# First expert's rows by one-hot products, router on un-normalised rows, bias split and table steps moved

## The reference, cut to what matters

```
h = h + mixed @ w_out
hn = rms_norm(h, norm_ffn_g)                       # h * rstd * g
logits = hn @ router_w + router_b
top_vals, top_idx = top_k(logits, 4); gates = softmax(top_vals)
# tokens sorted by expert, in blocks of 128
gu = x @ w_gate_up[e] + b_gate_up[e]
gate, lin = min(gu[:, 0::2], 7), clip(gu[:, 1::2], -7, 7)
act = gate * sigmoid(1.702 * gate) * (lin + 1)
y = act @ w_down[e] + b_down[e]                    # times the gate, added to h
```

## Time and profile before

| what | value |
|---|---|
| time, median of 3 runs | 1485.84 us (1485.42 to 1486.91) |
| profiled execution, its own time | 1486.37 us |
| its span | 1484.7 us |
| PE busy | 1418.3 us (96%) |
| DVE busy | 1235.6 us (83%) |
| ACT busy | 1006.7 us (68%) |
| POOL busy | 264.8 us (18%) |
| granted TensorE clock, mean | 0.966 |

### The profile page before, as it was taken

One profiled execution on the slowest core, in us unless ns is written; L12 is line 12 of the kernel. 1 busy time (PEld: TensorE's weight loads), 2 busy tenths in 40 slices (PEclk: granted clock), 3 DMA queues, 4 the chain that ended last, 5 costly groups with the idle time before them and its releaser, 6 DMA issues.

```text
span 1484.7 us, 20096 instructions
## 1 busy us (share of the span) xinstructions
PE 1418.3 (96%) x6498; PEld 1143.8 (77%) x6498; DVE 1235.6 (83%) x1074; ACT 1006.7 (68%) x1014; POOL 264.8 (18%) x280
## 2 busy tenths in 40 slices
PE   6998969879999999999999999999999999999995
PEld 4887447766888888888888888888888888888884
DVE  4688665566999999999989999999999999989994
ACT  5248265443777777777777777777777777777773
POOL 3000000054011112211211111122221122221111
PEclk9999979867999999999999999999999999999998
DMA  7412003658999999999999999999999999999971
GB/s 242 151 55 85 1 1 126 240 132 284 353 380 364 380 381 368 369 377 372 373 364 373 371 364 371 384 358 369 386 358 382 370 357 369 377 374 369 367 292 21
DMA packets 96842, 445.74 MB, mean 300 GB/s; under 512 B 14895, under 2 KB 19007, under 8 KB 63920
## 3 DMA queue, kind: packets, MB, share of 16 engines
q1 hardware_dynamic: 82752, 421.82, 75.2%
q0 software_dynamic: 11392, 17.61, 5.0%
q10 hardware_dynamic: 2672, 5.99, 1.3%
HBM read 439.96 MB, written 22.43 MB: 311 GB/s over the span
## 4 chain that ended last, share of the span: by engine, by line
PE 93%; DVE 3%; ACT 1%; DMA 1%; issue 1%; SPq 0%; POOL 0%; ACTq 0%; POOLq 0%; DVEq 0%
PE psum L1318 27%; PE psum L1319 27%; PE psum L1320 27%; PE psum L1609 2%; PE psum L1403 2%; PE psum L1618 2%; PE psum L1635 1%; DMA ring<-in_w_in 1%; PE psum L1644 1%; PE psum L1538 1%; PE psum L1476 1%; PE psum L1417 0%; DVE wlo L1215 0%; PE psum L1436 0%; PE psum L1556 0%
## 5 line engine op out<-in xcount | busy, mean ns | idle before, releaser
L1215 DVE TENSOR_TENSOR wlo<-ring,whi 128x2048 fp32r<-128x2048 f32 x384 | 871.6, 2290 | 109.7 <-ACT whi L783 105.9
L783 ACT ACTIVATE whi<-ring 128x2048 fp32r<-128x2048 f32 x384 | 737.2, 1920 | 195.0 <-PE psum L1320 195.0
L1318 PE MATMUL psum<-whi,xT_hi 128*128 128x512 f32 x1024 | 403.6, 394 | 6.2 <-DVE wlo L1215 3.4
L1319 PE MATMUL psum<-whi,xT_lo 128*128 128x512 f32 x1024 | 400.5, 391 | 0.0
L1320 PE MATMUL psum<-wlo,xT_hi 128*128 128x512 f32 x1024 | 400.3, 391 | 0.0
L1318 PEld LDWEIGHTS psum<-whi,xT_hi 128*128 128x128 f32 x1024 | 193.6, 189 | 46.7 <-DVE wlo L1215 3.8
L1320 PEld LDWEIGHTS psum<-wlo,xT_hi 128*128 128x128 f32 x1024 | 193.5, 189 | 40.5
L1319 PEld LDWEIGHTS psum<-whi,xT_lo 128*128 128x128 f32 x1024 | 193.6, 189 | 39.1
L1318 PE MATMUL psum<-whi,aT_hi 128*128 128x512 f32 x512 | 202.0, 395 | 1.9 <-ACT y_sb L809 1.9
L1320 PE MATMUL psum<-wlo,aT_hi 128*128 128x512 f32 x512 | 199.6, 390 | 0.0
L1319 PE MATMUL psum<-whi,aT_lo 128*128 128x512 f32 x512 | 199.5, 390 | 0.0
(11 more groups left out here) (241 smaller groups left out, 1356.4 us busy)
## 6 DMA issues: line engine op xcount, KB each, us to landing
ring<-in_w_gate_up SPq DMA_DIRECT2D x256, 1024.0 KB, 7.6
ring<-in_w_down SPq DMA_DIRECT2D x128, 1024.0 KB, 7.0
ring<-in_w_in SPq DMA_DIRECT2D x10, 1024.0 KB, 11.3
ring<-in_w_out SPq DMA_DIRECT2D x4, 1024.0 KB, 4.9
h<-in_x SPq DMA_DIRECT2D x4, 512.0 KB, 5.7
hn_rows<-hn ACTq DMA_DIRECT2D x4, 512.0 KB, 3.2
out<-h ACTq DMA_DIRECT2D x4, 512.0 KB, 8.2
bias_rows<-rows_st SPq DMA_DIRECT2D x1, 1280.0 KB, 4.8
```

Source lines behind the costliest of these rows:

```text
L783: nc.scalar.activation(whi[:, hi_of(number), :], ring[:, slot(number), :], ACT.Copy).then_inc(hi_ready, 1)
L1215: TT(wlo[:, slot(number), :], ring[:, slot(number), :], whi[:, hi_of(number), :].bitcast(F32), ALU.subtract).then_inc(lo_ready, 1)
L1318: MM(o, s_hi, m_hi, start=first, stop=False)
L1319: MM(o, s_lo, m_hi, start=False, stop=False)
```

## The change

- **Rows of item 0.** They are no longer gathered from HBM and transposed. DVE writes `sel_rows[:, t, :]` (128 x 128: token p of tile t is at place c of expert 0) and PE forms the transposed rows as `hn[:, t, d].T @ sel_rows[:, t]`, 8 float32 products of 128 columns for each tile. The gathers on POOL begin with item 1.
- **Router.** PE transposes `h1` instead of `hn`; `router_w` is multiplied by the norm's gain once (an extra small load, `gffn_k`), and `choose` multiplies the logits by `rstd2` while it adds the router's bias.
- **Ranks** are fp32r products of `mask_r`, `tri_r`, `ones_r`.
- **Up bias.** Loaded early on ACT's queue into ring slot 4, split (ACT line "b_split", DVE `bias_low` twice) into ring slot 5 between `add_rest(0)`, `(1)` and `(2)`, then moved by a POOL DMA to `b_hl`. Loads 10 and 11 of the ring wait for it.
- **Table steps, places, dense gates** come after `lo_item(0, 2)` and later, with the PE steps of them between the `use_up`; the transposes of the gates come after `bias_up(0)`, and ACT's evacuation of them after its last up chunk.

```diff
@@ ScalarE
             act.dma_start(g_ffn[:, :], norm_ffn_g.partition_broadcast(P)).then_inc(g_ffn_loaded, 16)
+            for part in range(4):
+                act.dma_start(b_raw[part * E:(part + 1) * E, :], b_gate_up).then_inc(braw_loaded, 16)
...
+            act.wait_ge(bhl_one, 1)
+            nc.scalar.activation(b_split[:, :], b_raw[:, :], ACT.Copy).then_inc(bhl_hi, 1)
             root(0)
             root(1)
...
             act.wait_ge(chunk_used, N_FRONT)
+            act.dma_start(b_dn[:, :], b_down).then_inc(b_dn_loaded, 16)
             gates_exp(1)
+            hi_item(0, 0)
+            hi_item(0, 1)
             gates_exp(2)
+            hi_item(0, 2)
             gates_exp(3)
...
-            for k in range(FIRST_HI):
+            xgT_out(0)
+            hi_item(0, FIRST_HI)
+            hi_item(0, FIRST_HI + 1)
+            for k in range(FIRST_HI + 2, UP):
                 hi_item(0, k)
             act.wait_ge(gdT_done, 1)
+            act.wait_ge(hn_stored, 16 * T)
-            nc.scalar.activation(gateT[:, :, :], bank(7)[0:E, :].rearrange("p (t c) -> p t c", t=T),
+            nc.scalar.activation(gateT[:, :, :], bank(4)[0:E, :].rearrange("p (t c) -> p t c", t=T),
                                  ACT.Copy).then_inc(gdT_evac, 1)
-            xgT_out(0)
-            act.wait_ge(braw_loaded, 80)
-            act.wait_ge(bhl_one, 1)
-            act.wait_ge(hn_stored, 16 * T)
-            nc.scalar.activation(b_hl[:, :], b_raw[:, :], ACT.Copy).then_inc(bhl_hi, 1)
-            for k in range(FIRST_HI, UP):
-                hi_item(0, k)
             hi_item(0, UP + 0)
             hi_item(0, UP + 1)
             sigmoid(0)
@@ VectorE
+            TT(rw[:, :, :], rw[:, :, :], gffn_k.unsqueeze(2).to_broadcast([P, KT, E]), ALU.mult).then_inc(rw_scaled, 1)
...
+            def position(t):
...
+                link(TT(pos[:, t, :], bank(RANKS[t])[:, 0:E], row_e[:, :], ALU.add))
+                TS(sel_rows[:, t, :], place_no[:, 0, :], pos[:, t, 0:1], mask[:, t, 0, 0:1], ALU.is_equal,
+                   ALU.mult).then_inc(rows_chosen, 1)
+            def next_lists():
+                for t in range(T):
+                    for e in range(1, AHEAD):
+                        TS(sel0[:, t, e - 1, :], place_no[:, e, :], pos[:, t, e:e + 1], mask[:, t, 0, e:e + 1], ALU.is_equal,
+                           ALU.mult).then_inc(sel0_ready, 1)
+            def one_more():
+                dve.wait_ge(braw_loaded, 64)
+                linear = b_raw[:, :].rearrange("p (f two) -> p two f", two=2)[:, 1, :]
+                TS(linear, linear, 1.0, None, ALU.add).then_inc(bhl_one, 1)
+            def bias_low(low):
+                dve.wait_ge(bhl_hi, 1)
+                TT(b_split[low, :], b_raw[low, :], b_split[low, :].bitcast(F32), ALU.subtract).then_inc(bhl_ready, 1)
+            one_more()
+            add_rest(0)
+            normalise(0)
+            bias_low(slice(E, 2 * E))
+            add_rest(1)
+            normalise(1)
+            bias_low(slice(3 * E, P))
+            add_rest(2)
+            normalise(2)
+            choose(0)
+            add_rest(3)
+            normalise(3)
+            position(0)
+            choose(1)
+            choose(2)
+            position(1)
+            choose(3)
+            position(2)
+            position(3)
+            lo_item(0, 0)
+            split_xgT(0)
+            lo_item(0, 1)
+            next_lists()
+            lo_item(0, 2)
+            dve.wait_ge(slot0_done, 1)
+            TS(slot0_i[:, 1:AHEAD], bank(4)[:, 497:496 + AHEAD], float(NOWHERE), None, ALU.add).then_inc(slot0_ready, 1)
...
+            lo_item(0, 3)
+            flags()
+            lo_item(0, 4)
+            place(0)
             places()
+            lo_item(0, 5)
+            place(1)
             items()
+            lo_item(0, 6)
+            place(2)
+            place(3)
+            dense_gates(0)
+            dense_gates(1)
+            pick(0, sel_up, sel_up_ready, None)
+            lo_item(0, 7)
+            dense_gates(2)
+            dense_gates(3)
             lo_item(0, UP + 0)
             clip(0)
@@ TensorE
+            def first_rows(t):
+                pe.wait_ge(rows_chosen, t + 1)
+                pe.wait_ge(hn_ready, t + 1)
...
+                for half in range(2):
+                    for k in range(4):
+                        d = (half * 4 + k) * P
+                        ins = MM(bank(6 + half)[:, k * P:(k + 1) * P], hn[:, t, d:d + P], sel_rows[:, t, :],
+                                 start=(t == 0 and k == 0), stop=(t == T - 1 and k == 3))
...
+            turn_h1(1)
             out_rows(3)
             ranks(0)
+            turn_h1(2)
             logits(1)
+            turn_h1(3)
+            logits(2)
             ranks(1)
             logits(3)
+            first_rows(0)
             ranks(2)
+            first_rows(1)
             ranks(3)
+            first_rows(2)
+            first_rows(3)
...
             pe.wait_ge(xgT_ready, 2)
             for k in range(UP):
                 use_up(0, k, k)
+                if k == 1:
+                    for t in range(T):
+                        first_slots_of(t)
+                if k == 2:
+                    counts()
+                if k == 3:
+                    prefix()
+                if k == 4:
+                    item_table()
+            pe.wait_ge(bhl_moved, 16)
             bias_up(0)
+            turn_gates()
+            pe.wait_ge(items_ready, 1)
+            pe.wait_ge(gdT_evac, 1)
+            pe.wait_ge(b_dn_loaded, 16)
             for t in range(T):
                 bias_down(t)
@@ GpSimd and SyncE
+            pool.wait_ge(logits_done, T)
+            pool.wait_ge(bhl_ready, 2)
+            pool.dma_start(b_hl[:, :], b_split[:, :]).then_inc(bhl_moved, 16)
+            pool.wait_ge(sel0_ready, T * (AHEAD - 1))
             nc.gpsimd.memset(xg[:, :], 0.0).then_inc(xg_cleared, 1)
             pool.wait_ge(slot0_ready, 1)
-            gather(0, slot0_i[:, 0:1])
-            scatter_rows(0)
-            scatter_rows(1)
             gather(1, slot0_i[:, 1:2])
-            scatter_rows(2)
-            scatter_rows(3)
+            for t in range(T):
+                scatter_rows(t)
             gather(2, slot0_i[:, 2:3])
...
                 if m == PER_ITEM - 3:
                     sp.wait_ge(hn_stored, 16 * T)
+                if m == PER_ITEM - 2:
+                    sp.wait_ge(bhl_ready, 2)
                 if m == PER_ITEM - 1:
-                    sp.wait_ge(xg_loaded, 16)
+                    sp.wait_ge(bhl_moved, 16)
```

More of the change, by code:

```diff
@@ L115, in build @@
         eps, spare = vecs[:, 23:24], vecs[:, 29:30]
+        gffn_k = vecs[:, 30:38]
         lam2, rlam = vecs[:, 24:26], vecs[:, 26:28]
@@ L450, in _ @@
                 small(sg, subln_g.rearrange("(p a) -> p a", a=1))
+                small(gffn_k, norm_ffn_g.rearrange("(k p) -> p k", p=P))
             small(rw[:, :, :], router_w.rearrange("(k p) e -> p k e", p=P))
@@ L754, in gates_exp, with hi_item @@
                                      accum_out=gates[:, t, 5:6]).then_inc(gate_exp, 1)
+            def hi_item(body, number):
+                act.wait_ge(slot_loaded[slot(number)], loads(body, number))
+                act.wait_ge(chunk_used, chunk(body, number) - HI + 1)
+                nc.scalar.activation(whi[:, hi_of(number), :], ring[:, slot(number), :], ACT.Copy).then_inc(hi_ready, 1)
             root(0)
@@ L1208, in _ @@
-            flags()
-            dense_gates(2)
-            dense_gates(3)
+            COPY(tri_r[:, :], tri[:, :])
+            COPY(ones_r[:, :], ones[:, :])
             def lo_item(body, number):
@@ L1552, in first_slots_of @@
             def first_slots_of(t):
[L1554 to L1557 removed]
+                for e in range(1, AHEAD):
+                    pe.wait_ge(sel0_ready, (AHEAD - 1) * t + e)
+                    ins = MM(bank(4)[:, 496 + e:497 + e], sel0[:, t, e - 1, :], token_no[:, t:t + 1],
+                             start=(t == 0 and e == 1), stop=(t == T - 1 and e == AHEAD - 1))
@@ L1577, in _ @@
             ranks(2)
-            first_slots_of(2)
+            first_rows(1)
             ranks(3)
-            first_slots_of(3)
-            for t in range(T):
-                ins = MM(bank(5)[0:96, 128:129], mask[:, t, :, :].rearrange("p r e -> p (r e)"), ones[:, 0:1],
-                         start=(t == 0), stop=(t == T - 1))
-            ins.then_inc(count_done, 1)
-            pe.wait_ge(flag_ready, 1)
-            MM(bank(6)[0:96, 128:129], tri[0:96, 0:96], f96[0:96, 0:1], start=True, stop=True).then_inc(prefix_done, 1)
@@ L1588, in _ @@
-            pe.wait_ge(tables_ready, 2)
-            pe.wait_ge(e96_ready, 8)
-            MM(bank(0)[:, 128:145], e96[:, :], f96[0:96, 4:21], start=True, stop=True)
-            MM(bank(0)[:, 160:177], r96[:, :], f96[0:96, 4:21], start=True, stop=True)
```

(15 more changed lines are left out.)

197 lines of the change are left out of this document (79 added, 118 removed).

## The result

The changed kernel takes 1488.88 us (median of 17 runs, 1485.35 to 1492.42), the kernel before 1485.84 (17 runs, 1484.37 to 1487.37): ratio 1.0022, 95% interval 1.0016 to 1.0029. It is a little slower, by 3.0 us, and not a little faster. The profiled execution of it took 1492.42 us (span 1490.8) and was the slowest of the 17; a second profile of the same kernel, of an execution of 1485.95 us, comes with the experiments.

What follows compares the result with a forecast made beforehand. PE, never idle from about 363 us, bounds the loop, so the change is worth what it moves the loop's start. 1486.37 - 12.2 + 10.8 = 1485.0, as median 1484.5; range 1478.5 to 1491.8.

Steps and rivals of the forecast that it cites:

- t0: Start of PE's first up product: 318.91 us before the change, forecast at 306.7, a gain of 12.2 us.
- the early bias: Before the first up product: up bias lands near 263 us beside the ring's loads, costing 2.3 us by `add_rest(3)`.
- R4: Slower rival: the bias lands late, at 271, moving `add_rest(0)` and all behind by 8 us: 1492.5; chance 0.10.
- Step 2: Router and first rows, from 285.5: clock falls near 290, returns about 300; first up product at 306.7, gaining 12.2 us.
- R1: Rival: PE's clock holds after 283, first up product at 302.3; 1479.5 us; chance 0.21.
- the two terms: Shift of the first up product (-12.2 us) and change from there to the second item's transposes (+10.8 us).
- R3: Slower rival: clock stays at half through `first_rows` and the first chunk, first up product at 312.3; 1491.6 us; chance 0.14.
- Step 3: From first up product to second item's transposes: 51.1 us against 40.3, through DVE's work and ACT's queue; 10.8 us lost.
- R2: Rival: ACT's queue or the bias costs less, landing by 260.5, evacuation hidden beside `bias_down(0)`; 1479.9 us; chance 0.13.
- Step 4: Small extra load, fp32r ranks, bias move on POOL's queue, gathers and 16 scatters: costed at nothing.

Runs made afterwards that it cites:

- the filler before `logits(0)`: Changed kernel plus 13 products of 512 columns nobody reads, between the third output rows and `logits(0)`; bias landing left late: 1487.76 us, ratio 1.0003.
- the fastest version: Changed kernel with bias loads during attention, two ACT roundings before gate evacuation, `place(0)`-`(2)` and `dense_gates(0)` earlier, three unread products before the last tile's transposes: 1471.36 us.
- the kernel with places early: Changed kernel with bias loads during attention, two ACT roundings before gate evacuation, `place(0)` to `(2)` and `dense_gates(0)` before the first low half: 1475.09 us.

## Why the prediction was wrong, point by point

The forecast was 1484.5, with faster or the same at 0.74 together; it is 1488.9 by median, inside the range and just past the 1488.8 from which the forecast counted it as slower. By the first profile, whose sum was to be 1485.0 and is 1492.4, the 7.4 us are, rounded, 5.1 up to `add_rest(3)`, 0.5 from there to t0, 1.2 from t0 to the transposes and 0.7 behind them.

**The step that failed is the first, the early bias: "landing near 263 ... Cost of this edit: 2.3 us at this point".** Five profiles with the loads where the change has them (one of them that with the filler before `logits(0)`) show `one_more` at 266.2, 264.6, 265.0, 266.6 and 265.6, and `add_rest(3)` beginning on average at 288.1, where the forecast's 285.5 for its end means 284.3: 3.8 us late, 5.1 in the slowest execution. Of the 3.8, 2.5 stand before `add_rest(0)`, which begins on average at 266.2 and not at 263.7, and 1.3 between it and `add_rest(3)`. Two parts of it:

- The rate. The sum let the two queues alternate from 255.5 on, 0.14 MB in each us for the bias. The queue shares (packets, MB, share), 255 to 257 and then 263 to 265:

```profile
q10 hardware_dynamic: 61, 0.32, 47.0%
...
q1 hardware_dynamic: 60, 0.39, 57.7%
...
q10 hardware_dynamic: 30, 0.11, 21.2%
...
q1 hardware_dynamic: 58, 0.48, 77.3%
```

  The first window agrees with the earlier trace rows, the last does not: the share of the bias's queue was 47.0, 27.4, 56.0, 23.9 and 21.2% in the five windows of 2 us, and it moved 1.10 MB in these 10 us, 0.11 in each. The split read in 253 to 255 did not last until the last packet. That leaves the landing some 2.6 us over the 263. Why the split changed is not shown.
- The clock. The forecast saw that "PE waits some 1.3 us for `logits(0)`" and priced it as waiting. With the later landing it was 3.12 us (1.54 in the second profile), and in both the clock then fell to half under `logits(0)`, the transposes and the start of `out_rows(3)`: 2.0 us more, by the filler experiment. With the clock held there, `add_rest(0)` to `add_rest(3)` took 20.56 us, and the forecast's own 263.7 to 284.3 is 20.6: the waits were priced rightly, and the fall of the clock stood at nothing.

R4 is the rival that held this mechanism. It had the price at one us for each us and the limit at a landing of 267; with the clock's part the limit lies lower: at 265.6 on average the change is already slower.

**Step 2, router and first rows.** In the first profile the sizes are as written: `first_rows(0)` at half clock (3.76, forecast 3.6), clock back near 305, that is 5 us after `first_rows(0)` starts; 22.87 us from `add_rest(3)` to t0, forecast 22.4. In the second the clock held, which is R1, and t0 was 307.02, all but the forecast's 306.7, though `add_rest(3)` was 4.5 us late. That is luck: the late bias (+4.5) and the clock that held (18.19 us to t0 and not 22.4, -4.2) cancelled, so that the two terms, -11.9 and +10.5 us, look as forecast (-12.2 and +10.8). The prediction calls the fall certain if the 16 transposes of the stretch help nothing; beside the same 16 transposes it did not come there. R3 did not come: the clock was back for the last two `first_rows` in every profile (3.82 us for the two, 3.97 in the fastest version).

**Step 3, from t0 on.** Last low half at t0 + 28.2 (forecast 28.3), last chunk at half clock, sigmoid at t0 + 40.7 (40.4), `clip` to t0 + 42.6 (41.7), transposes at t0 + 52.3 and 50.8 (51.1). The chain on ACT stood where the forecast had it. R2, that the queue costs less, is right in part: taking the queue away gave the changed kernel 1.5 us by median, since `bias_down` at half clock held the additions next, and the full 3.7 us and more only where `bias_down(0)` and `(1)` ran at full clock. R2's other half, a landing by 260.5, did not come.

**Step 4, the rest.** Costed at nothing, and the loop started with what it needed. The scatters took 1.36 us each on average against 1.83 in the earlier trace rows, where the forecast had them slower beside a denser DVE. What decides is not how busy DVE is but where a scatter begins. POOL's and DVE's timelines of the changed kernel:

```profile
332.44 2.82 POOL L505 DMA_INDIRECT slot_table<-payload,dest  x1 [0.30 <-issue]
...
338.13 0.98 POOL L505 DMA_INDIRECT slot_table<-payload,dest  x1 [0.30 <-issue]
```

```profile
331.93 2.27 DVE L1186 TENSOR_TENSOR wlo<-ring,whi 128x2048 fp32r<-128x2048 f32 x1
...
338.15 2.30 DVE L1186 TENSOR_TENSOR wlo<-ring,whi 128x2048 fp32r<-128x2048 f32 x1
```

The scatter at 332.44 begins inside a low half and ends 1.06 us after that has ended; the one at 338.13 begins 0.02 us ahead of one and takes 0.98 us. So it is for all 16 scatters in each of the thirteen profiles: one that begins inside a low half of 2.3 us (of a chunk or of the bias) ends 0.84 to 1.15 us behind its end and takes 1.9 to 3.0 us, every other takes 0.97 to 1.06. Before the change ten of the 16 began inside one, in the changed kernel four, because nine came behind the last low half of the up chunks, where DVE had one such operation left.

The Trainium skill, "SBUF — State Buffer", section "SBUF: two separate sides", has descriptor writes of POOL wait while DVE holds the shared ports. The scatters agree, with the numbers just given. The same section says that in a probe a `tensor_tensor` of DVE, unlike a copy, did not stall a DMA. These low halves are `tensor_tensor` subtractions with both operands in SBUF, and they held up an indirect DMA every time; the measurement decides.

**What stays open.** Why the clock holds through `logits(3)` in some executions of the same program and not in others. Both profiles had the first fall at 278 to 285, and from 289 to 295 PE ran the same products in the same order, 0.55 us apart. Nor is it shown why `bias_down(0)` and `(1)` ran at full clock in four profiles (3.67 to 3.78 us) and at half clock, for most of their time, in the others. The times of the changed kernel spread over 7 us and those of the kernel with places early over 1.5; that the clock makes all of that spread was not tried.

## What to carry to other kernels

A transfer that moves ahead of other work is priced by when its last packet lands beside the other queues, not by its share when it begins; issued before the ring's loads start, here 26 us earlier, it cost nothing. Idle time of PE on the critical path can cost twice, once for itself and once for the clock behind it: 12 or 3 products that nobody reads, put into such a gap, bought 3.1 and 3.7 us by median (1.5 and 2.9 in the stretch itself), 13 in a third gap nothing that the times can tell. When an edit moves work from before a mark to behind it, ask which engine bounds the new stretch and move other work of that engine back: four steps of DVE were worth 3.3 us. Whether a scatter of POOL is slow is read from what DVE runs when it begins, not from DVE's average share.

## What was not expected of the hardware

With two queues loading, the 16 engines were full but moved less. Shares in 259 to 261 of the changed kernel were 56.0% and 47.7% at 287 GB/s in all; the kernel before moved 410 GB/s there with one queue and 97.1%. The bias's packets did not only take turns with the ring's, the ring's became slower too: 0.26 MB in 47.7% of 2 us, against 0.82 MB in 97.1%.

`bias_down` is two float32 products of 512 columns over 32 rows for each tile (four records), eight for all four tiles and not eight for each. Its last two tiles took 7.19 us in nine of the twelve profiles taken with the change in, at half clock with PE busy throughout (in the changed kernel 357 to 363: 6.00 of 6 us, clock 0.50), with DVE's additions waiting for it. That stretch is the next one to look at.
